# A gated DeltaNet and sliding-window layer: the order of the small products in each head

## The chip, the cores and the metric

The kernel runs on one core of a Trainium2 chip. Its time is the device time of one launch in microseconds (us). The engines of the core are named as the profile names them: PE (TensorE, matmuls; PEld is its loading of stationary operands), DVE (VectorE), ACT (ScalarE), POOL (GpSimd), SP (SyncE, which issues most transfers). They run side by side, each through its own list of instructions in the order written, and wait for each other by semaphores.

## The reference, cut to what matters

One layer with 2048 tokens of width 1024. A normalised input is projected by one wide matrix; branch A is a gated delta rule with 8 heads, in chunks; branch B is attention over a window of two 64-token chunks, with a sink and a bias; both are gated, projected and added.

```python
n_mat = jnp.where(strict, -jnp.einsum('nbhid,nbhjd->nbhij', kb, kc) * decay, 0.0)
t_mat = jnp.eye(CHUNK) + n_mat
p_mat = n_mat
for _ in range(int(math.log2(CHUNK)) - 1):
    p_mat = jnp.einsum('nbhij,nbhjk->nbhik', p_mat, p_mat)
    t_mat = t_mat + jnp.einsum('nbhij,nbhjk->nbhik', t_mat, p_mat)
...
def step(state, inp):
    v_new = u_i - w_i @ state
    o_i = qg_i @ state + qk_i @ v_new
    state = state * jnp.exp(gl_i) + kd_i.T @ v_new
...
logits = einsum(q, k_band) * D ** -0.5 + bias        # 64 queries x 128 keys per chunk
m = jnp.maximum(jnp.max(logits, -1), sink)
p = jnp.exp(logits - m)
probs = p / (jnp.sum(p, -1) + jnp.exp(sink - m))
o = probs @ v_band
```

## The kernel before

The tokens are taken in 4 blocks of 512. Each block goes through 8 heads, so that there are 32 passes through the function `head`, which every engine has in its own version. In a head step the delta rule works on 4 tiles of 128 tokens (two chunks of 64 each), and the attention of one head pair on the block in two groups of 4 chunks: group 0 and group 1. The heavy work is the projection. It is split into steps: a step is three matmuls of 128x128 by 128x512 (lines 1275 to 1277, high and low parts of the operands), 8 steps make one weight tile, 6 tiles are one head's share. A generator yields after each step, and `fill(n)` in PE's `head` runs n steps of the projection of the next head between the small products of this one. The other engines have a `fill` of their own for the vector work that belongs to the next head. All orders are written out by hand.

The small products of one head, in PE's order before the change:

- decays, transposes and the products k·k and q·k; `fill(7)`; the transpose of the system matrix; `logits_padded` (group 0's logits, bank 3); `fill(11)`; `probs(0)` (group 0's probabilities transposed into bank 4, from where ACT copies them to `pts`).
- the inverse of the unit triangular matrices by repeated squaring, on 64x64 blocks, two blocks at a time: `square(l, g)` (line 1404) and `apply(l, g)` (line 1420) for the levels l = 1 to 5 and the tile pairs g = 0 and 1. After each `square` ACT copies the result (`p_ready`); after each `apply` DVE copies and adds it (line 843 `pt_ready`, line 1036 `tt_ready`). `apply(l, g)` waits for `tt_ready[g]` of the level before.
- `values(0)`, group 0's probabilities times values (line 1466, 128x64 operands, bank 3), and behind it the last `apply` (level 6), which needs DVE's line 1036 of level 5; it has no square.
- `fill(2)`; `merge_in` (lines 1428, 1429), which waits for `diag_ready`; `logits_quarters` (line 1451: group 1's logits, 64x64 operands, 128 columns, bank 3), which waits for `pv_read[0]`, DVE's reading of group 0's output; `merge_out` (line 1437), which waits for `t11_ready` (ACT's copy, line 718) and `z_ready` (DVE's copy, line 843), both copies of what `merge_in` made; `fill(2)`.
- four tiles t = 0 to 3 of the recurrence over the state, each with the products of lines 1498, 1503, 1513, 1519, 1522 and fills between them; tile 0 begins with line 1498 and has to wait for `full_ready` at its line 1513.

DVE's order around this place: the ten vector steps of the levels; `settled()` (line 843, four copies of 64x128), `diagonal()` (line 1051, four additions of 32x64, then `diag_ready`), `gated(0)` (line 1085, reads bank 3, `pv_read[0]`), the copy to `z_sb` (line 843, waits for `tz_done` of `merge_in`), `fill(1)` (line 954), `corner()` (line 843, waits for `t12_done` of `merge_out`), and `logits(1)` (lines 1065, 1072, 1073). Each matrix product with fp32 operands shows as two records in the trace, so that `values` has 16 records and half of an `apply` 8.

Of the kernel before, what the change touches and what calls it, by code (L numbers as in the profile page):

```python
# [6 lines left out]
P = 128  # L7
# [5 lines left out]
NT = TB // P  # L13
# [21 lines left out]
ALU = mybir.AluOpType  # L35
# [30 lines left out]
def bank_of(n):  # L66
    return GEMM[n] % 2


def reads_before(n):  # L70
    return GEMM[n] // 2
# [39 lines left out]
def build_program(nc, x, w_tiles, w_ba, norm_w, gdn_norm_w, decay_bias, step_const, bias, final_w, masks, saved, out):  # L111
    with ExitStack() as ctx:
        def sb(name, shape, dt=F32):
            return ctx.enter_context(nc.sbuf_tensor(name, shape, dt))

        def sem(name, n=None):
            if n is None:
                return ctx.enter_context(nc.semaphore(name))
            return [ctx.enter_context(nc.semaphore(f"{name}{i}")) for i in range(n)]
# [13 lines left out]
        kb = sb("kb", [P, CH + TB])  # L133
# [7 lines left out]
        qpl = sb("qpl", [P, NT, CH])  # L141
# [11 lines left out]
        bias_sb = sb("bias_sb", [P, 2, 2, P])  # L153
# [62 lines left out]
        lg = dec_n  # L216
# [26 lines left out]
        def bch(i):  # L243
            return bank[i][:, :].rearrange("p (t c) -> p t c", t=NT)


        def pv(b):
            return b[:, 0:NT * CH].rearrange("p (t c) -> p t c", t=NT)
# [103 lines left out]
        pts_ready = sem("pts_ready", 2)  # L352
        pv_done = sem("pv_done", 2)
        pv_read = sem("pv_read", 2)
# [484 lines left out]
        def _(dve):  # L839
            dve.wait_ge(zeroed, 5)  # L840

            def copy(dst, src):
                return dve.tensor_scalar(dst, src, 1.0, None, ALU.mult)  # L843
# [137 lines left out]
            def head(b, hh, fill):  # L981
                par, n1 = hh % 2, b * H + hh + 1
                n4, n6 = ((n1 - 1) * i for i in (NT, LEVELS + 1))
                ch = Chain(dve, dve_head, (n1 - 1) * DVE_HEAD)
# [20 lines left out]
                for t in range(NT):  # L1005
                    ins = dve.scalar_tensor_tensor(tt[:, t, :], bch(6)[:, t, :], bj[:, t:t + 1], dec_n[:, t, :],
                                                   ALU.mult, ALU.mult)
                ins.then_inc(f_ready, 1)
                dve.wait_ge(f_ready, n1)
                for lo, hi in HALVES:  # L1010
                    ins = dve.tensor_tensor(ptt[lo:hi, :, CH:P], tt[lo:hi, :, lo:hi],
                                            mk[lo:hi, IDENT:IDENT + 1, lo:hi].to_broadcast([CH, NT, CH]), ALU.add)
# [32 lines left out]
                def diagonal():  # L1045
                    ch.sync()
                    for g in range(2):
                        dve.wait_ge(a_done[g], n6 + (LEVELS + 1))
                        for lo, hi in HALVES:
                            part = slice(lo, lo + CH - LAST)  # L1050
                            ins = dve.tensor_tensor(tt[part, PAIR[g], lo + LAST:hi], bch(A_BANK[g])[part, PAIR[g], CH + LAST:P],
                                                    ptt[part, PAIR[g], CH + LAST:P], ALU.add)
                    ins.then_inc(diag_ready, 1)

                def corner():
                    dve.wait_ge(t12_done, n1)
                    copy(tt[0:CH, :, CH:P], bch(6)[0:CH, :, 0:CH]).then_inc(full_ready, 1)
# [3 lines left out]
                def logits(g):  # L1061
                    dve.wait_ge(lg_done[g], n1)
                    if g:
                        dve.wait_ge(prt_done[0], n1)
                        ch.inc(dve.tensor_tensor(lg, bch(3), bias_sb[:, par, 1:2, :].to_broadcast([P, NT, P]), ALU.add))
                    else:
                        dve.wait_ge(f_ready, n1)
                        ch.inc(dve.tensor_tensor(lg[:, 0, :], bank[3][:, 0:P], bias_sb[:, par, 0, :], ALU.add))
                        ch.inc(dve.tensor_tensor(lg[:, 1:NT, :], bch(3)[:, 1:NT, :],
                                                 bias_sb[:, par, 1:2, :].to_broadcast([P, NT - 1, P]), ALU.add))  # L1070
                    ch.sync()
                    ch.link(dve.tensor_reduce(mx[:, :], lg, AX, ALU.max))
                    dve.tensor_scalar(nmx[:, :], mx[:, :], sink, -1.0, ALU.max, ALU.mult).then_inc(nmx_ready[g], 1)  # L1073
# [7 lines left out]
                def gated(g):  # L1081
                    dve.wait_ge(z_read[bank_of(zb_n)], reads_before(zb_n) + 1)
                    dve.wait_ge(pv_done[g], n1)
                    part = slice(g * NT * CH, (g + 1) * NT * CH)
                    dve.tensor_tensor(zb[:, par, part], bank[3][:, 0:NT * CH], zb[:, par, part], ALU.mult).then_inc(pv_read[g], 1)

                logits(0)
                attention()
                fill(1)
# [5 lines left out]
                    level(l, 1)  # L1095
                settled()
                diagonal()
                gated(0)
                dve.wait_ge(tz_done, n1)
                copy(z_sb[0:CH], bch(5)[0:CH, :, 0:CH]).then_inc(z_ready, 1)  # L1100
                fill(1)
                corner()
                logits(1)
                dve.wait_ge(vr_ready, n1)
                for t in range(NT):
# [10 lines left out]
                    if b + 1 < NB or t + 1 < NT:  # L1116
                        dve.wait_ge(ds_done, state_steps(n1, t))
                        if b or t:
                            ins = dve.scalar_tensor_tensor(s_cur[:, (t + 1) % 2, :], s_cur[:, t % 2, :], sc[:, EGL, t:t + 1], bank[6][:, 0:P],  # L1119
                                                           ALU.mult, ALU.add)  # L1120
                        else:
                            ins = copy(s_cur[:, 1, :], bank[6][:, 0:P])
                        ins.then_inc(s_ready, 1)
                    dve.wait_ge(ay_done, n4 + (t + 1))
                    if b or t:
                        dve.wait_ge(o1_ready, read_steps(n1, t))
                        ins = dve.tensor_tensor(o_sb[:, t, :], bank[7][:, 0:P], o1_sb[:, t % 2, :], ALU.add)
                    else:
                        ins = copy(o_sb[:, 0, :], bank[7][:, 0:P])
# [39 lines left out]
            for b in range(NB):  # L1169
                b1 = b + 1  # L1170
                more = b + 1 < NB
                for h in range(H):
                    gen = project(b, h + 1) if h + 1 < H else iter(())

                    def fill(n):
                        for _ in range(n):
                            next(gen, None)
# [3 lines left out]
                for c in range(KT):  # L1181
# [3 lines left out]
                    n, g = USE["ya", b, c], USE["gate", b, 2 * c]  # L1185
# [13 lines left out]
                for c in range(KT):  # L1199
                    n, g = USE["yb", b, c], USE["gate", b, 2 * c + 1]  # L1200
# [50 lines left out]
                for half_n in range(2):  # L1251
                    dve.wait_ge(tile_done, USE["out", b, half_n * NT + NT - 1] + 1)
                    for t in range(NT):
                        half_row = y_out[:, t, half_n * TB:(half_n + 1) * TB]
                        ins = dve.tensor_tensor(half_row, bank[OUT_BANKS[half_n][t]][:, :], half_row, ALU.add)
# [8 lines left out]
                for t in range(NT):  # L1264
                    ins = dve.scalar_tensor_tensor(y_out[:, t, :], y_out[:, t, :], sty[:, 4 + t:5 + t], fw[:, :], ALU.mult, ALU.mult)
# [6 lines left out]
        def _(pe):  # L1272
# [93 lines left out]
            def head(b, par, n1, fill):  # L1366
# [15 lines left out]
                for dst, src, done in ((bch(6), k, kk_done), (bch(7), q, qk_done)):  # L1382
                    for t in range(NT):
                        c = slice(t * P, (t + 1) * P)
                        ins = pe.matmul(dst[:, t, :], k[:, c], src[:, c], start=True, stop=True)  # L1385
# [37 lines left out]
                def merge_in():  # L1423

                    pe.wait_ge(attn_ready, n1)
                    pe.wait_ge(diag_ready, n1)
                    for t in range(NT):
                        pe.matmul(bch(7)[0:CH, t, 0:CH], tt[0:CH, t, 0:CH], ident[0:CH, 0:CH], start=True, stop=True)
                        ins = pe.matmul(bch(5)[0:CH, t, 0:CH], od[CH:P, t, :], tt[CH:P, t, CH:P], start=True, stop=True)
                    ins.then_inc(tz_done, 1)  # L1430
# [13 lines left out]
                    ins.then_inc(lg_done[0], 1)  # L1444

                def logits_quarters():
                    pe.wait_ge(pv_read[0], n1)
                    for t in range(NT):
                        c = (NT + t) * CH
                        for lo, hi in HALVES:  # L1450
                            ins = pe.matmul(bch(3)[lo:hi, t, :], qpl[lo:hi, t, :], kb[lo:hi, c:c + P], start=True, stop=True)  # L1451
                    ins.then_inc(lg_done[1], 1)

                def probs(g):
# [6 lines left out]
                def values(g):  # L1461
                    pe.wait_ge(vwin_ready, (b + 1) * 2)
                    pe.wait_ge(pts_ready[g], n1)
                    for t in range(NT):
                        for lo, hi in ((0, CH), (CH, P)):
                            ins = pe.matmul(pv(bank[3])[lo:hi, t, :], vwin[:, g * NT + t, lo:hi], pts[:, t, lo:hi], start=True, stop=True)  # L1466
                    ins.then_inc(pv_done[g], 1)
# [4 lines left out]
                for t in range(NT):  # L1472
                    ins = pe.transpose(bch(5)[:, t, :], tt[:, t, :], ident)
# [4 lines left out]
                for l in range(1, LEVELS + 1):  # L1478
# [1 line left out]
                    apply(l, 0)  # L1480
                    square(l, 1)
                    apply(l, 1)
                values(0)
                apply(LEVELS + 1, 0)
                apply(LEVELS + 1, 1)
                fill(2)
                merge_in()
                logits_quarters()
                merge_out()
                fill(2)  # L1490
                for t in range(NT):
                    c = slice(t * P, (t + 1) * P)
                    if b or t:
# [37 lines left out]
                for t in range(NT):  # L1531
                    ins = pe.transpose(bch(4)[:, t, :], o_sb[:, t, :], ident)
# [26 lines left out]
            for b in range(NB):  # L1559
# [4 lines left out]
                for h in range(H):  # L1564
                    gen = project(b, h + 1) if h + 1 < H else gates(b)

                    def fill(n):
                        for _ in range(n):
                            next(gen, None)
# [24 lines left out]
                for half_n in range(2):  # L1594
                    for q in range(NT):
# [6 lines left out]
                        for t in range(NT):  # L1602
# [8 lines left out]
                            for kk in range(2):  # L1611
                                k = 2 * q + kk
                                c = slice(t * P, (t + 1) * P)
                                wc = slice(kk * TB, (kk + 1) * TB)
                                ins = split_mm(bank[OUT_BANKS[half_n][t]][:, :], oa_hi[:, k, c], oa_lo[:, k, c],
                                               w_sl[:, s, 0, wc], w_sl[:, s, 1, wc], k == 0, k == KT - 1)
# [100 lines left out]
```

## Time and profile before

| what | value |
|---|---|
| time, median of 3 runs | 2742.23 us (2742.21 to 2742.46) |
| the profiled execution | 2742.61 us, its span 2740.8 us |
| PE busy | 2709.1 us, 99% of the span |
| DVE, ACT, POOL busy | 1416.8, 973.9, 398.9 us |
| chain of work that ended last | 97% of the span on PE |
| lines 1275 to 1277 in that chain | 24% each |
| mean granted clock of PE | 0.999 of full speed |
| DMA | 458.43 MB, 167 GB/s on average |

A matmul is counted as busy from its start to its modelled end, and matmuls overlap: a projection matmul shows 0.39 us, and the next starts about 0.23 us after it. So a short wait of PE does not show as idle time. It shows in the distance from one start to the next, which is what the timeline gives.

### The profile page before, as it was taken

How to read it: one execution, taken by the hardware profiler on the slowest of the kernel's cores; microseconds unless marked ns; L12 is line 12 of the kernel's file. 1: busy time of each engine (PE TensorE's matmuls, PEld its weight loads, DVE VectorE, ACT ScalarE, POOL GpSimd, SP SyncE). 2: the span in 40 equal slices, each digit the busy share in tenths (PEclk: the TensorE clock that was granted, in tenths of full speed). 3: DMA queues.
4: the chain of work that ended last, by engine and by line, in shares of the span. 5: the costliest groups of instructions: out<-in, count | busy, mean ns of one | idle time of the engine just before them, and what ended most of it. 6: DMA issues, size and time to landing. Idle time of an engine off the chain costs nothing.

```text
span 2740.8 us, 50319 instructions
## 1 busy us (share of the span) xinstructions
PE 2709.1 (99%) x19808; PEld 2290.5 (84%) x19808; DVE 1416.8 (52%) x3631; ACT 973.9 (36%) x3156; POOL 398.9 (15%) x238
## 2 busy tenths in 40 slices
PE   7999999999999999999999999999999999999998
PEld 6888888888888888888888888888888888888887
DVE  6677777223366666612236666661224666665012
ACT  4554555422243444321124444432112344444101
POOL 3333343343100100000000101000000010000000
PEclk9999999999999999999999999999999999999999
DMA  7554455687733333355553233325546333333564
GB/s 245 182 192 166 167 180 189 241 286 278 262 125 113 112 124 123 113 195 206 183 217 128 101 120 126 128 98 211 213 172 218 111 116 125 122 111 120 182 221 169
DMA packets 79001, 458.43 MB, mean 167 GB/s; under 512 B 13232, under 2 KB 17456, under 8 KB 31792
## 3 DMA queue, kind: packets, MB, share of 16 engines
q1 hardware_dynamic: 65088, 425.75, 43.5%
q10 hardware_dynamic: 13680, 29.46, 3.1%
q8 instruction: 160, 2.62, 0.4%
q14 instruction: 73, 0.60, 0.1%
HBM read 352.42 MB, written 102.76 MB: 166 GB/s over the span
## 4 chain that ended last, share of the span: by engine, by line
PE 97%; DVE 1%; DMA 1%; issue 0%; ACTq 0%; POOL 0%; DVEq 0%; ACT 0%; SPq 0%; POOLq 0%
PE bank L1275 24%; PE bank L1277 24%; PE bank L1276 24%; PE bank L1420 5%; PE bank L1404 3%; PE bank L1385 2%; PE bank L1373 2%; PE bank L1466 1%; PE bank L1513 1%; PE bank L1458 1%; PE bank L1451 1%; PE bank L1443 1%; PE bank L1522 1%; PE bank L1519 1%; PE bank L1503 1%; PE bank L1498 1%
## 5 line engine op out<-in xcount | busy, mean ns | idle before, releaser
L1275 PE MATMUL bank<-hT_hi,w_sl 128*128 128x512 f32 x2112 | 873.0, 413 | 0.0
L1277 PE MATMUL bank<-hT_hi,w_sl 128*128 128x512 f32 x2112 | 826.5, 391 | 0.0
L1276 PE MATMUL bank<-hT_lo,w_sl 128*128 128x512 f32 x2112 | 824.7, 390 | 0.0
L1277 PEld LDWEIGHTS bank<-hT_hi,w_sl 128*128 128x128 f32 x2112 | 396.5, 188 | 87.1
L1275 PEld LDWEIGHTS bank<-hT_hi,w_sl 128*128 128x128 f32 x2112 | 398.0, 188 | 71.5 <-issue 1.2
L1276 PEld LDWEIGHTS bank<-hT_lo,w_sl 128*128 128x128 f32 x2112 | 398.6, 189 | 65.5 <-issue 0.7
L427 POOL TENSOR_TENSOR w_sl<-w_raw,w_sl 128x1024 fp32r<-128x1024 f32 x90 | 217.8, 2424 | 401.2 <-ACT w_sl L505 401.2
L954 DVE SCALAR_TENSOR_TENSOR area<-zraw,stc,area 128x512 f32<-128x512 f32 x288 | 220.4, 765 | 4.2
L1420 PE MATMUL bank<-area 64*64 64x128 f32 (+3 forms) x3072 | 197.7, 245 | 0.1
L843 DVE TENSOR_SCALAR area<-bank 128x128 f32<-128x128 f32 (+1 forms) x328 | 103.7, 316 | 158.9 <-PE bank L1420 115.5
L1420 PEld LDWEIGHTS bank<-area 64*64 64x64 f32 x3072 | 146.2, 134 | 2.8 <-issue 0.4
L1119 DVE SCALAR_TENSOR_TENSOR s_cur<-s_cur,scs,bank 128x128 f32<-128x128 f32 x112 | 39.0, 348 | 200.6 <-PE bank L1519 200.6
L1404 PE MATMUL bank<-area 64*64 64x64 f32 (+1 forms) x2560 | 138.7, 221 | 3.8 <-issue 0.6
L446 POOL TENSOR_TENSOR gu<-mk,g_hi 128x512 fp32r<-128x512 f32 x32 | 42.8, 1337 | 646.2 <-DVE nmx L1073 605.9
L594 ACT ACTIVATE area<-area 128x512 f32<-128x512 f32 x96 | 60.5, 630 | 186.8 <-DVE area L954 186.8
L677 ACT ACTIVATE area<-bank 128x128 f32<-128x128 f32 (+1 forms) x320 | 85.2, 266 | 111.5 <-PE bank L1404 108.6
L1404 PEld LDWEIGHTS bank<-area 64*64 64x64 f32 x2560 | 109.8, 133 | 17.2 <-issue 12.6
L505 ACT ACTIVATE w_sl<-w_raw 128x1024 fp32r<-128x1024 f32 x90 | 95.1, 1058 | 77.6 <-PE bank L1277 47.2
L440 POOL TENSOR_TENSOR rqo<-qo,half 128x8 f32<-128x8 f32 x32 | 52.4, 1638 | 438.9 <-DVE qo L1144 438.9
L1188 DVE SCALAR_TENSOR_TENSOR area<-area,bank 128x512 f32<-128x512 f32 x28 | 19.3, 688 | 159.6 <-PE bank L1277 159.6
L727 ACT ACTIVATE y_sb<-bank 128x128 f32<-128x128 f32 x128 | 35.6, 278 | 185.0 <-PE bank L1513 185.0
L1275 PE MATMUL bank<-oa_hi,w_sl 128*128 128x512 f32 x256 | 100.6, 393 | 0.2 <-DMA w_sl<-saved_w 0.2
(222 smaller groups left out, 4627.5 us busy)
## 6 DMA issues: line engine op xcount, KB each, us to landing
w_sl<-saved_w SPq DMA_DIRECT2D x270, 1024.0 KB, 4.8
saved_w<-w_sl SPq DMA_DIRECT2D x90, 1024.0 KB, 4.8
w_raw<-in_w_tiles SPq DMA_DIRECT2D x90, 512.0 KB, 5.9
area<-in_x ACTq DMA_DIRECT2D x4, 2048.0 KB, 10.0
area<-in_x ACTq DMA_DIRECT2D x14, 512.0 KB, 8.0
out_y<-area ACTq DMA_DIRECT2D x3, 2048.0 KB, 8.6
bias_sb<-in_bias ACTq DMA_DIRECT2D x32, 128.0 KB, 2.2
out_y<-area ACTq DMA_DIRECT2D x4, 512.0 KB, 3.0
```

The source lines that it names most:

```text
L427: pool.tensor_tensor(w_sl[:, s, 1, :], w_raw[:, f % 2, :], w_sl[:, s, 0, :].bitcast(F32), ALU.subtract).then_inc(lo_ready, 1)
L505: act.activation(w_sl[:, s, 0, :], w_raw[:, f % 2, :], ACT.Copy).then_inc(hi_ready, 1)
L594: act.activation(ez[i % 2], qkv[:, par, i, :], ACT.Tanh, scale=0.5).then_inc(tanh_z[i], 1)
L677: act.activation(p_sb[l % 2][:, PAIR[g], 0:width], pv(bank[P_BANK[g]])[:, PAIR[g], 0:width], ACT.Copy).then_inc(p_ready[g], 1)
L843: return dve.tensor_scalar(dst, src, 1.0, None, ALU.mult)
L954: ins = dve.scalar_tensor_tensor(acc, zraw[:, i, k:k + TB], stc[:, par, CONV * i + k:CONV * i + k + 1], acc, ALU.mult, ALU.add)
L1275: pe.matmul(dst, a_hi, b_hi, start=first, stop=False)
L1276: pe.matmul(dst, a_hi, b_lo, start=False, stop=False)
L1277: return pe.matmul(dst, a_lo, b_hi, start=False, stop=last)
L1373: ins = pe.transpose(bch(2 + i)[:, t, :], src[:, t * P:(t + 1) * P], ident)
L1404: ins = pe.matmul(pv(bank[P_BANK[g]])[lo:hi, t, 0:width], ptt[lo:hi, t, 0:CH], p_sb[(l - 1) % 2][lo:hi, t, 0:width], start=True, stop=True)
L1420: ins = pe.matmul(bch(A_BANK[g])[lo:hi, t, c0:c1], p_sb[(l - 1) % 2][lo:hi, t, :], ptt[lo:hi, t, c0:c1], start=True, stop=True)
```

## The change

On PE, behind the last `apply`, the two projection steps go, and the order becomes `logits_quarters`, `merge_in`, `values(0)`, `merge_out`, with four projection steps behind them in place of two. Group 1's logits are written to bank 4 instead of bank 3, and wait only for `pts_ready[0]` (ACT's copy out of bank 4); the wait for `pv_read[0]` moves to `values(1)`. On DVE `gated(0)` moves behind the copy to `z_sb`, and `corner()` ahead of `fill(1)`. No product is added or left out, and the number of projection steps in a head is the same.

```diff
@@ DVE, logits(g)
-    ch.inc(dve.tensor_tensor(lg, bch(3), bias_sb[...], ALU.add))
+    ch.inc(dve.tensor_tensor(lg, bch(4), bias_sb[...], ALU.add))
@@ DVE, head
     settled()
     diagonal()
-    gated(0)
     dve.wait_ge(tz_done, n1)
     copy(z_sb[0:CH], bch(5)[0:CH, :, 0:CH]).then_inc(z_ready, 1)
+    gated(0)
+    corner()
     fill(1)
-    corner()
     logits(1)
@@ PE, logits_quarters
-    pe.wait_ge(pv_read[0], n1)
+    pe.wait_ge(pts_ready[0], n1)
...
-    ins = pe.matmul(bch(3)[lo:hi, t, :], qpl[lo:hi, t, :], kb[lo:hi, c:c + P], start=True, stop=True)
+    ins = pe.matmul(bch(4)[lo:hi, t, :], qpl[lo:hi, t, :], kb[lo:hi, c:c + P], start=True, stop=True)
@@ PE, values(g)
     pe.wait_ge(pts_ready[g], n1)
+    if g:
+        pe.wait_ge(pv_read[0], n1)
@@ PE, head
-    values(0)
     apply(LEVELS + 1, 0)
     apply(LEVELS + 1, 1)
-    fill(2)
+    logits_quarters()
     merge_in()
-    logits_quarters()
+    values(0)
     merge_out()
-    fill(2)
+    fill(4)
```

## Rows read from the trace of the kernel before

**Rows 1.** The page: busy time of PE, and its granted clock in 40 slices.

```profile
PE 2709.1 (99%) x19808; PEld 2290.5 (84%) x19808; DVE 1416.8 (52%) x3631; ACT 973.9 (36%) x3156; POOL 398.9 (15%) x238
...
PEclk9999999999999999999999999999999999999999
```

**Rows 2.** Waits of PE: who for whom, us in total, times, longest.

```profile
PE bank L1513 <- DVE r_sb L1108: 2.1, 7, 0.3
```

**Rows 3.** Timeline of PE in head 21: start, length of the group, line, records.

```profile
1674.12 0.42 PE L1404 MATMUL bank<-area 64*64 64x32 f32 x8
1674.34 0.44 PE L1420 MATMUL bank<-area 64*64 64x48 f32 x8
1674.71 0.69 PE L1466 MATMUL bank<-area,vwin 128*64 128x64 f32 x16
1675.33 0.66 PE L1420 MATMUL bank<-area 64*64 64x32 f32 x16
1675.91 0.50 PE L1275 MATMUL bank<-hT_hi,w_sl 128*128 128x512 f32 x1
1676.25 0.39 PE L1276 MATMUL bank<-hT_lo,w_sl 128*128 128x512 f32 x1
...
1677.18 0.40 PE L1277 MATMUL bank<-hT_hi,w_sl 128*128 128x512 f32 x1
...
1677.52 0.27 PE L1429 MATMUL bank<-area 64*64 64x64 f32 x1
...
1677.97 0.22 PE L1429 MATMUL bank<-area 64*64 64x64 f32 x1
1678.02 1.04 PE L1451 MATMUL bank<-kb,qpl 64*64 64x128 f32 x15
1678.90 0.62 PE L1437 MATMUL bank<-area 64*64 64x64 f32 x8
1679.45 0.50 PE L1275 MATMUL bank<-hT_hi,w_sl 128*128 128x512 f32 x1
...
1680.95 0.38 PE L1498 MATMUL bank<-s_cur,area 128*128 128x128 f32 x2
...
1682.09 0.39 PE L1275 MATMUL bank<-hT_hi,w_sl 128*128 128x512 f32 x1
...
1682.99 0.39 PE L1276 MATMUL bank<-hT_lo,w_sl 128*128 128x512 f32 x1
```

**Rows 4.** Timeline of DVE in head 21, with idle time before and its releaser.

```profile
1673.68 0.29 DVE L843 TENSOR_SCALAR area<-bank 128x128 f32<-128x128 f32 x1 [0.18 <-PE bank L1420]
...
1674.82 0.26 DVE L1036 TENSOR_TENSOR area<-bank,area 128x96 f32<-128x96 f32 x1 [0.41 <-PE bank L1420]
1675.00 0.92 DVE L843 TENSOR_SCALAR area<-area 64x128 f32<-64x128 f32 x4
1675.95 0.91 DVE L1051 TENSOR_TENSOR area<-bank,area 32x64 f32<-32x64 f32 x4
1676.89 0.42 DVE L1085 TENSOR_TENSOR zb<-bank,zb 128x256 f32<-128x256 f32 x1
1678.24 0.42 DVE L843 TENSOR_SCALAR area<-bank 64x256 f32<-64x256 f32 x1 [0.92 <-PE bank L1429]
1678.58 0.73 DVE L954 SCALAR_TENSOR_TENSOR area<-zraw,stc,area 128x512 f32<-128x512 f32 x1
1679.56 0.42 DVE L843 TENSOR_SCALAR area<-bank 64x256 f32<-64x256 f32 x1 [0.25 <-PE bank L1437]
```

**Rows 5.** Timeline of ACT in head 21.

```profile
1674.58 0.22 ACT L677 ACTIVATE area<-bank 128x64 f32<-128x64 f32 x1 [0.45 <-PE bank L1404]
...
1678.24 0.38 ACT L718 ACTIVATE area<-bank 64x256 f32<-64x256 f32 x1 [2.95 <-PE bank L1429]
```

**Rows 6.** The last head, 32: timelines of DVE and of PE.

```profile
2516.95 0.91 DVE L1051 TENSOR_TENSOR area<-bank,area 32x64 f32<-32x64 f32 x4
...
2518.53 0.27 PE L1429 MATMUL bank<-area 64*64 64x64 f32 x1
```

More of the change, by code:

```diff
@@ L1064, in logits @@
                         dve.wait_ge(prt_done[0], n1)
-                        ch.inc(dve.tensor_tensor(lg, bch(3), bias_sb[:, par, 1:2, :].to_broadcast([P, NT, P]), ALU.add))
+                        ch.inc(dve.tensor_tensor(lg, bch(4), bias_sb[:, par, 1:2, :].to_broadcast([P, NT, P]), ALU.add))
                     else:
```

## The prediction, made before the changed kernel was run

> **What bounds the kernel now.** I read the page first: PE is busy 99% of the span, the next engine 52%, and PE's clock stands at full speed in every slice, which is the upper of its two levels, 2.4 GHz [rows 1]. So the end is set by PE, and the change adds and removes no product. It can act only through when PE starts each product. The list of waits shows almost nothing for PE in the heads, the largest entry being 2.1 us over the run [rows 2]. That is not the whole truth, because records overlap: a projection matmul is 0.39 to 0.40 us long and the next one starts 0.23 us later. A wait shorter than that overlap is no idle time in the table. The view that prices this change is therefore the timeline of one head, read from start to start [rows 3]. I took head 21, in the middle of the run. The last head has the same distance from DVE's line 1051 to PE's line 1429: 2518.53 - 2516.95 = 1.58 us against 1677.52 - 1675.95 = 1.57 us [rows 3, 4, 6]. So one head, times 32, is the answer.
>
> **How the stretch runs before.** The last product of level 5 starts as its group ends, less one record: 1674.34 + 0.44 - 0.22 = 1674.56. Line 1466 (`values(0)`) starts at 1674.71, the level 6 products at 1675.33, the two projection steps at 1675.91, `merge_in` at 1677.52, `logits_quarters` at about 1677.97, `merge_out` at 1678.90, the second two steps at 1679.45, and tile 0 with line 1498 at 1680.95 [rows 3]. The end I compare is the start of line 1498. Everything behind it is unchanged work.
>
> **Part 1: two changes of operand shape less.** Going from 64x64 products to the 128x128 projection and back costs time. In: 1675.91 follows the last level 6 start (1675.33 + 0.66 - 0.22 = 1675.77) by 0.14 us, where the 16 starts within that group come as eight pairs 0.06 apart (0.44 us over seven steps), so 0.08; the first projection matmul then keeps the second back 0.34 us instead of 0.23, so 0.11. Out: 1677.18 to 1677.52 is 0.34 instead of 0.23, so 0.10, and the first pair adds about 0.04. Together 0.33 us a head, 10.6 us over 32 heads, gained [rows 3]. `values(0)` still lies between 64x64 products, so its two edges stay: 0.15 us from the last 64x64 start to its first, and 0.62 us from its start to the next group's.
>
> The Trainium skill speaks to this term ("TensorEngine Tiling (Array Packing)", Key Properties): a change of tiling mode, not of tile, drains TensorE. The trace agrees with it, at 0.14 to 0.15 us instead of 0.06 at such an edge. If only that rule worked here, the sum would be the 10.6 us gained and nothing else.
>
> **Part 2: what those steps and `values(0)` covered.** Three waits lay behind them.
>
> First, `apply(6, 1)`. It needs DVE's line 1036 of level 5, which ends at 1674.82 + 0.26 = 1675.08; it also needs ACT's copy, done at 1674.80 [rows 4, 5]. DVE's work starts from level 5's product, so it does not move. Before, `values(0)` filled this time. How long after DVE's end does PE start? In the levels DVE's line 843 ends at 1673.68 + 0.29 = 1673.97 and PE's line 1404, which needs it, starts at 1674.12: 0.15 us [rows 3, 4]. So `apply(6, 1)` starts at 1675.23 now, while `apply(6, 0)`, 8 records from 1674.62 on, has let PE go by about 1674.88: a hole of 0.35 us. Its 8 records take 0.22 us as line 1404's do, so `logits_quarters` starts at 1675.45. It needs 0.90 us with its handover (1678.90 - 1677.97 = 0.93 with the edge), and PE is free for `merge_in` at about 1676.35.
>
> Second, `merge_in`. It waits for `diagonal()`. DVE's chain is line 1036 to 1675.08, four copies from 1675.00 to 1675.92, four additions from 1675.95 to 1676.86, each following the other without a hole, and none of them waits for level 6 even now: those products are done at 1675.45 + 0.22, before the additions begin [rows 4]. With 0.15 us to hand over, `merge_in` starts at 1677.01. PE stands from 1676.35 to 1677.01, 0.66 us, and the first hole is swallowed in it: the position of `merge_in` is set by DVE alone. What stands behind PE's wait is everything, as PE is one queue: `values(0)`, which has been ready for long, is written behind `merge_in` and can't fill the hole.
>
> Third, `merge_out`. `merge_in` has its last start 0.45 us after its first (1677.52 to 1677.97), so at 1677.46. It ends 0.22 us later, 1677.68, and both copies begin 0.05 us behind it (before: 1677.97 + 0.22 = 1678.19, then 1678.24). DVE is free then, as `gated(0)` now stands behind the copy. The DVE copy takes 0.42, ACT's 0.38 [rows 4, 5], so `z_ready` comes at 1678.15 and `merge_out` can start at 1678.30. `values(0)` covers this: it starts 0.15 us after `merge_in`'s last start, at 1677.61, and 0.62 us later, at 1678.23, PE is ready. The wait left is 0.07 us.
>
> **The sum for a head.** `merge_out` starts at 1678.30 and the projection 0.55 us behind it (1678.90 to 1679.45), at 1678.85. Two steps then lead to line 1498 in 1.50 us (1679.45 to 1680.95). Two more are six matmuls at 0.225 to 0.233 us (0.90 us for four, 1682.09 to 1682.99; 0.93 us for four, 1676.25 to 1677.18): 1.37 us [rows 3]. Line 1498 starts at 1678.85 + 1.50 + 1.37 = 1681.72, where it started at 1680.95: 0.77 us later. Seen the other way: 0.33 us gained from the edges, some 1.1 us lost in the three holes of 0.35, 0.66 and 0.07.
>
> 32 heads x 0.77 = 24.6 us. The profiled execution is 2742.61 us, with 1.8 us around its span of 2740.8, and the median is 2742.23, 0.4 us under it. The sum is a difference, so I put it on the median: **2766.8 us**, 0.9% slower.
>
> **What costs nothing.** Bank 4 is free for the second logits: ACT has copied it before level 1, long before. `probs(1)` writes it much later, behind DVE's reading. `gated(0)` on DVE: `values(0)` ends about 1678.34, it runs to 1678.80, and `corner()`, which waits for `merge_out` to about 1678.95, is not held up; if it were, `full_ready` has six projection matmuls and tile 0's fills to hide in. DVE's line 954 then starts at about 1679.3 instead of 1678.58; ACT's next use of it stands just before its work for tile 0, which needs line 1503, behind line 1498 at 1681.72; about 1 us of cover remains when both have run. `logits(1)` ends at about the same absolute time, while PE is 0.77 us later, so it waits for less. POOL's only link is the same `nmx` result. No transfer is issued at another place: SP's refills hang on finished projection tiles, and no tile boundary lies in the two moved steps (they are steps 19 and 20; tiles end at 16 and 24). The new wait in `values(1)` is for something done a whole recurrence earlier.
>
> **Bounds.** The handover from DVE to PE is the one price that I carry over. Below, the shortest handover in the rows is 0.05 us (PE to DVE); with 0.05 both times `merge_in` starts at 1676.91 and `merge_out` at 1678.13, behind `values(0)`, and the head loses 0.60 us, 19 us in all. Above, a handover of 0.25 us both times gives 0.97, 31 us. The value taken is 0.15 because it is the same pair of engines in the same direction. The waits of rows 2 (2.1 us) could vanish, at most 2 us less. So the likeliest case alone spans 2759 to 2773 us.
>
> **The rivals.**
>
> *The edges win (faster).* If DVE's chain did not end last, only Part 1 is left, and the time would be 2742.2 - 10.6 = 2731.6 us. It decides from the point where `diag_ready` comes before 1676.20, that is 0.66 us earlier than DVE's rows end. For it speaks that PE's waits are near zero today. Against it stand the eight DVE instructions, 1.86 us back to back from 1675.00 to 1676.86 [rows 4], none of which the change shortens or starts earlier. Chance 0.03.
>
> *Gain and loss balance (same).* That needs holes of only 0.33 us, a DVE chain 0.77 us shorter or a hole that is paid back within the head, because PE waits somewhere in the recurrence for DVE anyway. The rows of waits leave 2.1 us of such waits in the whole run. Chance 0.03.
>
> *The clock falls in the holes (much slower).* PE would have new pauses of up to 0.66 us. If that took it to the lower level over, say, the four steps behind, their 2.87 us would double, 92 us more in all, about 2859 us. Against it: in the levels PE already waits for DVE again and again (line 1404 starts 0.15 us behind the end of DVE's line 843 [rows 3, 4]), and the clock stays full in every slice [rows 1]. Chance 0.01.
>
> *Slower as worked out*: 0.93.
>
> The range is that of the likeliest case, 2759 to 2773 us, as the others hold less than 2 in 10. By the cases: faster 0.03, same 0.03, slower 0.94, where 0.2% (5.5 us) is about what a measurement of this kernel can tell from no change.
>
> **What the changed profile would show.** Line 1429's first start 0.15 us after the end of line 1051's group, and line 1466 behind it; from the last level 5 start to line 1429's first 2.45 us, against 2.96 before; the first start of line 1451 some 0.9 us behind that level 5 start; line 1498 at 7.16 us, against 6.39 before. A new entry in PE's waits: the matmul of line 1429 (or its load) released by DVE's line 1051, 32 times. The prediction would be wrong if DVE's additions came earlier, if the handover were far from 0.15 us, or if the recurrence gave time back.

## The result: 0.9% slower, and the profile after

The changed kernel takes 2768.14 us (median of 4 runs, 2766.90 to 2768.27) against 2742.35 us for the kernel before (2742.21 to 2743.65): 25.8 us more, a ratio of 1.0091 with a 95% interval of 1.0079 to 1.0103. Forecast were 2766.8 us and a range of 2759 to 2773. The profiled execution took 2768.17 us, its span is 2766.4 us against 2740.8. (One of the experiments below, the last, was profiled in an execution whose clock was granted at 0.753 throughout; only the times of its other runs are used.)

The page answers [rows 1] with PE hardly busier in us, but in a longer span, at the same clock.

```profile
span 2766.4 us, 50319 instructions
...
PE 2711.7 (98%) x19808; PEld 2294.7 (83%) x19808; DVE 1414.4 (51%) x3631; ACT 972.7 (35%) x3156; POOL 397.4 (14%) x238
...
PEclk9999999999999999999999999999999999999999
```

The waits of PE, which had 2.1 us as their largest entry inside the heads [rows 2], have two new ones, both on DVE. The columns are: who waited for whom, us in all, how often, the longest.

```profile
PE bank L1428 <- DVE area L1051: 14.1, 31, 0.5
PE bank L1328 <- DMA db<-in_decay_bias: 13.9, 1, 13.9
PE bank L1420 <- DVE area L1036: 6.5, 30, 0.2
...
PE bank L1514 <- DVE r_sb L1108: 1.9, 7, 0.3
```

The two on lines 1036 and 1051 add up to 20.6 us of idle time, less than the holes are long, because the last record before each hole is still counted as running for 0.22 to 0.27 us. The timeline of PE in head 21 shows the true length (compare [rows 3]; line 1466 is now 1468, and 1498 is 1499):

```profile
1690.32 0.42 PE L1404 MATMUL bank<-area 64*64 64x32 f32 x8
1690.55 0.66 PE L1420 MATMUL bank<-area 64*64 64x48 f32 x16
1691.43 0.42 PE L1420 MATMUL bank<-area 64*64 64x32 f32 x8 [0.22 <-DVE area L1036]
1691.66 1.10 PE L1451 MATMUL bank<-kb,qpl 64*64 64x128 f32 x16
1693.21 0.24 PE L1428 MATMUL bank<-mk,area 64*64 64x64 f32 x1 [0.46 <-DVE area L1051]
...
1693.67 0.22 PE L1429 MATMUL bank<-area 64*64 64x64 f32 x1
1693.82 0.69 PE L1468 MATMUL bank<-area,vwin 128*64 128x64 f32 x16
1694.49 0.65 PE L1437 MATMUL bank<-area 64*64 64x64 f32 x8
1695.07 0.50 PE L1275 MATMUL bank<-hT_hi,w_sl 128*128 128x512 f32 x1
...
1697.92 0.38 PE L1499 MATMUL bank<-s_cur,area 128*128 128x128 f32 x2
```

DVE in the same head (compare [rows 4]):

```profile
1691.03 0.26 DVE L1036 TENSOR_TENSOR area<-bank,area 128x96 f32<-128x96 f32 x1 [0.41 <-PE bank L1420]
1691.20 0.92 DVE L843 TENSOR_SCALAR area<-area 64x128 f32<-64x128 f32 x4
1692.15 0.91 DVE L1051 TENSOR_TENSOR area<-bank,area 32x64 f32<-32x64 f32 x4
1693.93 0.42 DVE L843 TENSOR_SCALAR area<-bank 64x256 f32<-64x256 f32 x1 [0.87 <-PE bank L1429]
1694.62 0.42 DVE L1085 TENSOR_TENSOR zb<-bank,zb 128x256 f32<-128x256 f32 x1 [0.28 <-PE bank L1468]
1695.18 0.42 DVE L843 TENSOR_SCALAR area<-bank 64x256 f32<-64x256 f32 x1
1695.52 0.73 DVE L954 SCALAR_TENSOR_TENSOR area<-zraw,stc,area 128x512 f32<-128x512 f32 x1
```

The reader is to see three things. The two large holes of PE end 0.14 to 0.15 us behind an end of DVE: 1691.03 + 0.26 = 1691.29, then 1691.43; 1692.15 + 0.91 = 1693.06, then 1693.21. DVE's own chain has the same lengths as before: 0.26, 0.92 and 0.91 us, back to back. And the distance that matters, from the start of the last `square` (line 1404) to the start of tile 0's first product, is 1697.92 - 1690.32 = 7.60 us, where it was 1680.95 - 1674.12 = 6.83 [rows 3]: 0.77 us a head, 24.6 us in 32 heads, of the 25.6 us between the spans. Most of the last 1.0 us lies in the same place: the same distance read in each of the 32 heads and added up is 25.3 us longer than before (in the first 8 heads, which have no line 1498 in tile 0, up to the next product that is not projection). I call the distance in head 21 the **stretch** below. Each experiment but the last is read by it, version 7 from further ahead.

### The profile page after: what moved, and what is told of

Same layout as the page of the kernel before. It is cut to its first block, busy times and chain, and to the rows that moved or that the text cites. A ratio compares the mean times of both kernels' runs of the same rounds, so it can differ in the third digit from the quotient of the medians.

```text
span 2766.4 us, 50319 instructions
## 1 busy us (share of the span) xinstructions
PE 2711.7 (98%) x19808; PEld 2294.7 (83%) x19808; DVE 1414.4 (51%) x3631; ACT 972.7 (35%) x3156; POOL 397.4 (14%) x238
## 4 chain that ended last, share of the span: by engine, by line
PE 95%; DVE 3%; DMA 1%; issue 1%; ACTq 0%; POOL 0%; DVEq 0%; ACT 0%; SPq 0%; POOLq 0%
PE bank L1275 24%; PE bank L1277 23%; PE bank L1276 23%; PE bank L1420 4%; PE bank L1404 3%; PE bank L1385 2%; PE bank L1373 2%; PE bank L1468 1%; PE bank L1514 1%; PE bank L1443 1%; PE bank L1458 1%; DVE area L1051 1%; PE bank L1523 1%; PE bank L1520 1%; PE bank L1504 1%; PE bank L1499 1%
## 5 line engine op out<-in xcount | busy, mean ns | idle before, releaser
L446 POOL TENSOR_TENSOR gu<-mk,g_hi 128x512 fp32r<-128x512 f32 x32 | 36.7, 1148 | 648.1 <-DVE nmx L1073 608.1
```

## The experiments

Times are medians. The kernel before ran beside them, at 2742.71 us (first four) and 2742.58 us (last four). The changed kernel was not run again, so comparisons with it use the 2768.14 us of above. Ratios are to the kernel before, with their 95% interval.

**1. The first hole closed.** The changed kernel with `values(0)` put back ahead of level 6:

```diff
+values(0)
 apply(LEVELS + 1, 0)
 apply(LEVELS + 1, 1)
 logits_quarters()
 merge_in()
-values(0)
 merge_out()
 fill(4)
```

> The changed kernel with values(0) put back ahead of the level 6 products, which closes the 0.35 us hole in front of apply(6, 1). Chain theory (merge_in starts 0.15 us behind DVE's last addition whatever PE does before, and merge_out 0.82 us behind merge_in's last start): nothing moves, line 1498 stays at 7.16 us behind the last level 5 start, and the time stays at 2768 us, within 2 us. Rival (the three holes add up, so closing one pays): 0.35 us a head less, 11 us, 2757 us.

Measured: 2766.95 us (ratio 1.0076 to 1.0103), as the expectation from DVE's chain had it. The timeline of its PE, head 21:

```profile
1688.39 0.42 PE L1404 MATMUL bank<-area 64*64 64x32 f32 x8
...
1690.09 1.07 PE L1451 MATMUL bank<-kb,qpl 64*64 64x128 f32 x16
1691.27 0.24 PE L1428 MATMUL bank<-mk,area 64*64 64x64 f32 x1
...
1692.56 0.65 PE L1437 MATMUL bank<-area 64*64 64x64 f32 x8 [0.60 <-DVE area L843]
...
1695.98 0.38 PE L1499 MATMUL bank<-s_cur,area 128*128 128x128 f32 x2
```

The hole in front of `apply(6, 1)` is gone, the second logits start earlier, and `merge_in` still comes 2.88 us behind the last square, as in the changed kernel (2.89). PE's idle time has only changed its place: 0.60 us now stand in front of `merge_out`, which `values(0)` no longer covers. `merge_out` starts 0.82 us behind `merge_in`'s last start here (1691.74 to 1692.56) as in the changed kernel (1693.67 to 1694.49). The stretch is 7.59 us. So the holes don't add up: the starts of `merge_in` and of `merge_out` are both set by DVE, and closing what lies between them buys nothing.

**2. Two of the four projection steps back ahead of `merge_in`**, behind the second logits (`fill(2)` there, `fill(2)` at the end).

> The changed kernel with two of its four projection steps back in front of merge_in, behind the second logits; values(0) stays behind merge_in. Chain theory: the long hole is filled and both edges are paid again; what is left is the hole in front of apply(6, 1) and 0.07 us in front of merge_out, so 0.42 us a head over the kernel before, 13 us, 2756 us. Rival (the loss comes from bank 4 or from DVE's new order, not from the lost cover): still about 2768 us.

Measured: 2758.57 us (1.0043 to 1.0070), expected 2756. Stretch 7.33 us (1684.33 to 1691.66). The wait on line 1051 is gone from its list of waits; the one on line 1036 stays with 6.5 us. The stretch is 0.50 us over the 6.83 of before, where 0.42 was expected; the 0.08 us point to the edges, which cost more here (see experiment 6).

**3. The whole order of PE back, bank 4 and DVE's new order kept.**

> PE's order of the kernel before (values(0), level 6, two steps, merge_in, second logits, merge_out, two steps), with the second logits in bank 4 and DVE in the changed order (gated(0) behind the copy to z_sb, corner ahead of fill). Chain theory: the time of the kernel before, 2742.3 us, within 2 us. Rival (bank 4 and DVE's order cost something by themselves): over 2748 us.

Measured: 2742.58 us (0.9991 to 1.0009). Stretch 6.83 us (1674.01 to 1680.84). In PE's old order neither the other bank nor the moved DVE instructions cost anything. The loss comes with PE's order.

**4. One pair of edges more.** The kernel before with its last `fill(2)` split, one step ahead of `merge_out` and one behind.

```diff
 logits_quarters()
+fill(1)
 merge_out()
-fill(2)
+fill(1)
```

> The kernel before with its last two steps split: one between the second logits and merge_out, one behind merge_out. It adds one pair of edges between 64x64 and 128x128 operands and no wait. If a pair is worth the 0.33 us that the distances of starts give: 10.6 us more, 2753 us. Rival (an edge costs nothing, since matmuls overlap): 2742 us. Rival (an edge costs a whole emptied array, 0.5 us a pair or more): 2758 us or more.

Measured: 2753.91 us (1.0027 to 1.0052), 11.2 us more. The stretch is 7.18 us, 0.35 more than 6.83. The forecast read 0.33 us for the pair that the change takes out, from the distances of starts. The pair added here shows the same distances:

```profile
1683.65 1.04 PE L1451 MATMUL bank<-kb,qpl 64*64 64x128 f32 x15
1684.61 0.50 PE L1275 MATMUL bank<-hT_hi,w_sl 128*128 128x512 f32 x1
1684.95 0.40 PE L1276 MATMUL bank<-hT_lo,w_sl 128*128 128x512 f32 x1
1685.18 0.39 PE L1277 MATMUL bank<-hT_hi,w_sl 128*128 128x512 f32 x1
1685.50 0.67 PE L1437 MATMUL bank<-area 64*64 64x64 f32 x8
1686.11 0.50 PE L1275 MATMUL bank<-hT_hi,w_sl 128*128 128x512 f32 x1
```

Beside [rows 3], the way from the logits to the next group takes 0.96 us instead of 0.88, the first projection matmul 0.34 instead of 0.23, the last 0.32 instead of 0.23, and `merge_out` to the projection 0.61 instead of 0.55: 0.34 us in all.

**5 and 6. DVE's chain made shorter.** The changed kernel with two, and with three, of the four additions of `diagonal()` left out, so that the inverse is not completed in those blocks:

```diff
 for g in range(2):
     dve.wait_ge(a_done[g], n6 + (LEVELS + 1))
-    for lo, hi in HALVES:
+    for lo, hi in (HALVES if g else ()):        # 5;  6: (HALVES[1:] if g else ())
```

> The changed kernel, with two of DVE's four additions in diagonal() left out (those of the first tile pair, so part of the inverse is not completed). DVE's chain ends 0.45 us earlier. Chain theory: merge_in starts 0.45 us earlier, at 2.00 us behind the last level 5 start, and all behind it too: 14 us less than the changed kernel, 2753 us. Rival (the loss is PE's own: edges, the hole at apply(6, 1) or the four steps in a row): no change from 2767 us.

> The changed kernel, with three of DVE's four additions left out (part of the inverse is not completed). DVE's chain ends 0.68 us earlier, just when PE has finished the second logits. Chain theory: merge_in starts at 1.78 to 1.80 us, about 0.65 us earlier, 21 us less than the changed kernel, 2746 us; what then stays over the kernel before is the hole at apply(6, 1) and 0.07 us less the pair of edges, 0.1 us a head. Rival (the pair of edges is worth nothing): the 0.33 us of it is missing only in the comparison with the kernel before, which would then be 0.4 us a head better, so 2755 us and more.

Measured: 2751.78 us with two left out (1.0024 to 1.0050) and 2745.25 us with three (1.0001 to 1.0019), 16.4 and 22.9 us below the changed kernel, where 14 and 21 were expected. The stretches are 7.14 and 6.91 us (1676.28 to 1683.19), 0.46 and 0.69 below 7.60, for additions that took 0.46 and 0.69 us (0.91 less the 0.45 and 0.22 that are left). DVE's time comes back one for one in PE's place. With three left out the stretch is still 0.08 us over the 6.83 of before, 2.6 us in 32 heads, and 2.7 us are measured. That agrees with the remainder of the forecast's sum: holes of about 0.35 and 0.07 us against one pair of edges of 0.33. The rows of experiment 6, PE and then DVE:

```profile
1676.28 0.42 PE L1404 MATMUL bank<-area 64*64 64x32 f32 x8
...
1677.61 1.10 PE L1451 MATMUL bank<-kb,qpl 64*64 64x128 f32 x16
1678.48 0.27 PE L1429 MATMUL bank<-area 64*64 64x64 f32 x1
...
1683.19 0.38 PE L1499 MATMUL bank<-s_cur,area 128*128 128x128 f32 x2
```

```profile
1678.11 0.22 DVE L1051 TENSOR_TENSOR area<-bank,area 32x64 f32<-32x64 f32 x1
```

`merge_in` follows the last start of the logits (1677.61 + 1.10 - 0.27 = 1678.44) without a pause. In experiment 2 it doesn't wait for DVE either, and the two kernels differ there by one pair of edges: 7.33 - 6.91 = 0.42 us, and 13.3 us between the measured times. So a pair of edges between the second logits and `merge_in` costs 0.42 us, more than the 0.35 of experiment 4. Part of it is the way in: the first projection matmul starts 0.20 us behind the last of the logits in experiment 2 (1686.49 to 1686.69), where it is 0.14 behind level 6 [rows 3].

**7 and 8. A version for speed.** In the levels PE waits for DVE too, twice for longer than usual. In the kernel before, the groups of levels 1 to 2 start as follows:

```profile
1668.12 0.45 PE L1404 MATMUL bank<-area 64*64 64x64 f32 x8
1668.40 0.40 PE L1420 MATMUL bank<-area 64*64 64x64 f32 x8
1668.63 0.40 PE L1404 MATMUL bank<-area 64*64 64x64 f32 x8
1668.87 0.40 PE L1420 MATMUL bank<-area 64*64 64x64 f32 x8
1669.36 0.45 PE L1404 MATMUL bank<-area 64*64 64x64 f32 x8
```

Four groups follow each other by 0.23 to 0.28 us, and `square(2, 0)` comes after 0.49. The second logits are 64x64 products like their neighbours, so they can stand there without an edge, and with bank 4 they are free early enough. Version 7 cuts them up over the waits:

```diff
 for l in range(1, LEVELS + 1):
+    if l == 2:
+        logits_quarters((0,))
     square(l, 0)
     apply(l, 0)
+    if l == LEVELS:
+        logits_quarters((1,))
     square(l, 1)
     apply(l, 1)
 apply(LEVELS + 1, 0)
+logits_quarters((2, 3))
 apply(LEVELS + 1, 1)
-logits_quarters()
+fill(2)
 merge_in()
 values(0)
 merge_out()
-fill(4)
+fill(2)
```

Version 8 has all four tiles between `apply(6, 0)` and `apply(6, 1)` and none in the levels.

> A version for speed, same result: the second logits (64x64 products in bank 4, no edge) are cut up and put where PE waits for DVE: one tile ahead of square(2, 0), where the start distance is 0.31 us, one ahead of square(5, 1), where it is 0.22, two between apply(6, 0) and apply(6, 1). Two projection steps are back ahead of merge_in, values(0) covers merge_in's copies. The number of edges is that of the kernel before. Chain theory: merge_in at 2.65 us, line 1498 at about 6.0 us behind the last level 5 start instead of 6.38: 0.37 us a head less than the kernel before, 12 us, 2731 us. Rival (PE's distances in the levels are its own issue time and not waits for DVE, so pieces put there lengthen them): about 2742 us or more.

> As the version before it, but with all four tiles of the second logits between apply(6, 0) and apply(6, 1) and none in the levels. The hole there is 0.35 us, the products 0.85 us long, so 0.5 us of them lies open; no other hole is left. Chain theory: line 1498 at 6.41 us, the time of the kernel before, 2743 us. The difference to the version before it, 0.4 us a head or 12 us, is then what the level waits can hide. Rival as there: equal to it.

Measured: version 7 takes 2730.81 us, a ratio to the kernel before of 0.9958 (0.9945 to 0.9970): 11.8 us faster than before and 37.3 us faster than the change. Version 8 takes 2744.82 us (0.9998 to 1.0016), so the pieces in the level waits are worth 14.0 us, where 12 were expected. Version 7's timeline of PE, head 21:

```profile
1661.78 0.45 PE L1404 MATMUL bank<-area 64*64 64x64 f32 x8
...
1662.53 0.40 PE L1420 MATMUL bank<-area 64*64 64x64 f32 x8
1662.76 0.39 PE L1451 MATMUL bank<-kb,qpl 64*64 64x128 f32 x4
1663.02 0.45 PE L1404 MATMUL bank<-area 64*64 64x64 f32 x8
...
1668.48 0.66 PE L1451 MATMUL bank<-kb,qpl 64*64 64x128 f32 x8
1668.95 0.40 PE L1420 MATMUL bank<-area 64*64 64x32 f32 x8
...
1674.23 0.38 PE L1505 MATMUL bank<-s_cur,area 128*128 128x128 f32 x2
```

`square(2, 0)` starts 0.49 us behind `apply(1, 1)` here too (1662.53 to 1663.02), with four records of the logits between them: this piece is free. From level 1's first product to tile 0's it is 1674.23 - 1661.78 = 12.45 us, against 1680.95 - 1668.12 = 12.83 before. The 0.38 us are 12.2 us over 32 heads. The 37.3 us between the change and version 7 come in three parts: two projection steps back ahead of `merge_in` (experiment 2) 9.6 us, the second logits in the hole of level 6 (version 8 against experiment 2) 13.7, and the pieces in the levels 14.0.

## Why the prediction was right, point by point

- *PE's order in one head, times 32, is the whole answer.* Shown: experiment 3 gives the old time back by PE's order alone, and the stretch of the changed kernel and of experiments 1 to 6, less 6.83 us and times 32, lies within 1.2 us of the measured difference to the kernel before. For version 7 the distance from level 1 on does so within 0.4 us; version 8 is not read this way.
- *The edges are worth 0.33 us a head.* Borne out in size, but not measured at the very place: a pair elsewhere cost 0.35 us (experiment 4) and 0.42 us (experiment 2 against 6), and the 0.33 fit what is left in experiment 6. The rule of the Trainium skill that was weighed there ("TensorEngine Tiling (Array Packing)", Key Properties: a change of tiling mode drains TensorE) agrees with the runs in that a change costs time; whether the cost is a drain no run shows. The pair is too small to outweigh the cover.
- *`apply(6, 1)` stands 0.35 us.* The hole is there: the last start ahead of it is 1690.55 + 0.66 - 0.22 = 1690.99 (the second half of these 16 records is level 6), 0.44 us before 1691.43, where 0.06 is the usual distance. That makes 0.38 us.
- *`merge_in` starts 0.15 us behind DVE's last addition, at 2.89 us behind the last square.* 1693.21 - 1690.32 = 2.89 (forecast 1677.01 - 1674.12 = 2.89). The handover is 0.15 us, the one price carried over. Shown as a cause by experiments 2, 5 and 6.
- *`merge_out` waits 0.07 us for the copy.* It starts 0.67 us behind `values(0)`, where 0.62 is the length without a wait, so it waits 0.05. Its place is 4.17 us behind the last square (forecast 4.18), 0.14 us behind the copy's end at 1694.35. That its wait is as large as 0.60 us without `values(0)` is seen in experiment 1.
- *Bank 4, `gated(0)`, `corner()`, line 954 and the moved steps cost nothing.* Shown together by experiment 3, but for the moved steps: for them it is only argued, from the heads adding up to 25.3 of 25.6 us. Line 954 starts at 5.20 us behind the last square, as forecast.
- *The clock stays.* The page's row of it is full, in spite of holes of two thirds of a us.

Three things were put too simply. PE's waits name line 1051 31 times, not 32. And the list of holes, 0.35 and 0.66 and 0.07, reads as if they could be closed one at a time; experiment 1 shows that the first can't be sold by itself. The sum itself went by DVE's chain, and so was not hurt. Last, the rival *the edges win* has the time fall to 2731.6 us once `diag_ready` comes 0.66 us earlier. In experiment 6 the additions end 0.69 us earlier, and the kernel still takes 2745.25 us, more than before: the holes in front of `apply(6, 1)` and `merge_out` stay, and eat up the edges. The rival needed these two gone as well.

## What to carry to other kernels

A long filler between two dependent groups is worth its edges as long as the other engine's chain beneath it is longer than what could stand there instead: here 1.4 us of projection and `values(0)` covered a DVE chain of 2.0 us, and the projection's edges cost 0.33. Before joining like products, lay the other engine's chain beside the new order, and look for work that fits into the waits without an edge; the same products, cut up and put where PE waited anyway, with two projection steps back as cover, turned 25.8 us lost into 11.8 us gained. And read a saturated engine from start to start: this PE was "99% busy" and stood still in every head.

## What the runs showed of the hardware

- The handover from DVE's end to the next matmul's start was 0.14 to 0.15 us at each of the three places of the changed kernel (head 21): 0.14 behind line 1036, 0.15 behind the additions, 0.14 behind the copy.
- A wait of PE of 0.3 us can show as no idle time at all. In experiment 1 `merge_in` starts 0.38 us behind the last start of the logits (1690.09 + 1.07 - 0.27 = 1690.89, then 1691.27), where 0.06 is the usual distance, and neither the timeline nor the list of waits has an entry for it. In the changed kernel the last start ahead of `merge_in` is at 1691.66 + 1.10 - 0.27 = 1692.49, 0.72 us before 1693.21, so that the wait is 0.66 us; the timeline has 0.46 for it.
- A pair of edges between 64x64 and 128x128 operands took 0.34 to 0.35 us between the second logits and `merge_out` (experiment 4): 0.19 going into the projection, 0.15 coming out. Between the second logits and `merge_in` it took 0.42 us (experiment 2 against 6).
